# Two of the eight TensorE steps of the second modulation group are placed one wait earlier

## The reference, cut to what matters

```python
mod = jax.nn.silu(c) @ w_ada + b_ada                      # 1024 -> 6 * 1024
sh1, sc1, g1, sh2, sc2, g2 = split(mod, 6)
h = rms_norm(x, norm1_g) * (1 + sc1) + sh1
proj = h @ w_in                                            # qa, ka, va, qb, kb, vb, gates
qa, ka = rope(rms_norm(qa)), rope(rms_norm(ka))
for gi, (win, dil) in enumerate(DIL_GROUPS):               # 3 groups of 4 heads, head width 64
    o, l = dilated_window_attention(qa, ka, va, win, dil)
oa = sum(softmax(lses) * outs)                             # "first attention" of the kernel
ob = differential_attention(q1, q2, k1, k2, vb, lam)       # "second attention", 8 heads
x = x + g1 * ((gates_a * (oa @ w_proj_a) + gates_b * (ob @ w_proj_b)) @ w_out)
```

## Time and profile before

| what | us |
|---|---|
| median of three runs | 1869.84 |
| the profiled execution's own time | 1871.05 |
| its span, first to last instruction | 1869.3 |
| TensorE busy | 1827.0 |
| VectorE busy | 1371.7 |
| ScalarE busy | 912.0 |

### The profile page before, as it was taken

The page is one execution under the profiler, slowest core; times in us unless marked ns, Lnnn a source line. Parts: engine busy times, 40 slices in busy tenths (PEclk is TensorE's granted clock), DMA queues, the critical chain, the costliest instruction groups (busy, mean ns, idle before and its releaser), DMA issues.

```text
span 1869.3 us, 24560 instructions
## 1 busy us (share of the span) xinstructions
PE 1827.0 (98%) x9392; PEld 1530.4 (82%) x9392; DVE 1371.7 (73%) x1903; ACT 912.0 (49%) x1013; POOL 77.6 (4%) x101
## 2 busy tenths in 40 slices
PE   8999999999999999999999999999999999999998
PEld 4778766888899877888888888889988888888886
DVE  5679588669998665666666666667875688888897
ACT  2553465311334444444444444456645467667675
POOL 0000000100000431110000000000000000000000
PEclk9999899999999999999999999999999999999999
DMA  7655365434446785666555555555343589898884
GB/s 310 247 181 201 113 225 192 158 125 147 163 153 229 248 275 188 212 210 222 182 200 180 196 185 191 190 184 191 143 143 127 219 312 360 319 354 325 340 342 183
DMA packets 61697, 404.94 MB, mean 217 GB/s; under 512 B 8129, under 2 KB 8417, under 8 KB 15281
## 3 DMA queue, kind: packets, MB, share of 16 engines
q1 hardware_dynamic: 51904, 371.22, 54.2%
q0 software_dynamic: 5968, 20.82, 3.9%
q10 hardware_dynamic: 3746, 11.83, 1.9%
HBM read 391.25 MB, written 12.58 MB: 216 GB/s over the span
## 4 chain that ended last, share of the span: by engine, by line
PE 84%; DVE 7%; DMA 3%; ACT 3%; issue 1%; DVEq 0%; ACTq 0%; SPq 0%
PE ps L2339 18%; PE ps L2341 17%; PE ps L2340 17%; PE ps L2733 9%; PE ps L2451 7%; PE ps L2735 4%; PE ps L2761 3%; DVE wlo L1241 2%; DMA raw<-in_stream_dram 2%; ACT whi L693 2%; DMA BIG<-in_stream_dram 1%; PE ps L2942 1%; PE ps L2461 1%; PE ps L2563 1%; PE ps L2584 1%
## 5 line engine op out<-in xcount | busy, mean ns | idle before, releaser
L1241 DVE TENSOR_TENSOR wlo<-raw,whi 128x2048 fp32r<-128x2048 f32 x179 | 410.2, 2292 | 201.3 <-ACT whi L693 201.1
L693 ACT ACTIVATE whi<-raw 128x2048 fp32r<-128x2048 f32 x179 | 343.0, 1916 | 375.7 <-PE ps L2341 190.3
L2733 PE MATMUL ps<-tboth,whi 128*128 128x512 f32 x736 | 259.8, 398 | 0.0
L2339 PE MATMUL ps<-whi,phi 128*128 128x512 f32 x608 | 238.9, 393 | 6.2 <-DVE plo L1832 6.2
L2341 PE MATMUL ps<-whi,plo 128*128 128x512 f32 x608 | 237.4, 391 | 0.0
L2340 PE MATMUL ps<-wlo,phi 128*128 128x512 f32 x608 | 237.4, 391 | 0.0
L2339 PE MATMUL ps<-whi,tboth 128*128 128x512 f32 (+1 forms) x576 | 226.7, 394 | 7.0 <-DVE wlo L1241 4.2
L2341 PE MATMUL ps<-whi,tboth 128*128 128x512 f32 (+1 forms) x576 | 223.1, 387 | 0.0
L2340 PE MATMUL ps<-wlo,tboth 128*128 128x512 f32 (+1 forms) x576 | 223.0, 387 | 0.0
L2735 PE MATMUL ps<-tboth,wlo 128*128 128x256 f32 x644 | 181.0, 281 | 0.0
L2451 PE MATMUL ps<-h2T,raw 128*128 128x256 f32 x768 | 172.4, 380 | 0.0
(11 more groups left out here) (426 smaller groups left out, 3074.7 us busy)
## 6 DMA issues: line engine op xcount, KB each, us to landing
raw<-in_stream_dram SPq DMA_DIRECT2D x259, 1024.0 KB, 4.8
BIG<-in_stream_dram SPq DMA_DIRECT2D x84, 1024.0 KB, 6.6
BIG<-g_spill POOLq DMA_DIRECT2D x64, 128.0 KB, 4.8
BIG<-in_stream_dram SPq DMA_DIRECT2D x2, 2048.0 KB, 16.3
spare<-in_stream_dram SPq DMA_DIRECT2D x4, 1024.0 KB, 7.2
g_spill<-H ACTq DMA_DIRECT2D x4, 1024.0 KB, 4.8
g_spill<-MOD ACTq DMA_DIRECT2D x4, 1024.0 KB, 4.8
MID<-in_gains_dram POOLq DMA_DIRECT2D x7, 512.0 KB, 4.0
```

What stands on the lines that cost most here:

```text
L693: nc.scalar.activation(whi[:, u % 2, :], raw_of(u), ACT.Copy).then_inc(unit_hi, 1)
L1241: nc.vector.tensor_tensor(wlo[:, u % 2, :], raw_of(u), whi[:, u % 2, :].bitcast(f32), ALU.subtract).then_inc(unit_split, 1)
L2339: nc.tensor.matmul(out, ahi, bhi, start=start, stop=False)
L2733: last = nc.tensor.matmul(out, whi[:, s, cols], both, start=c == 0, stop=c == DC - 1)
```

## The change

`ada_half(1, 0)`, which stood behind the first two scores, now stands ahead of them, right behind the last transposes of q and k, with a wait for the copy that frees bank 7. `ada_half(1, 1)`, which stood in step 0 of the loop, takes the old place of `ada_half(1, 0)`. In the loop, step i now issues `ada_half(1, i + 2)` in place of `ada_half(1, i + 1)`, and step 6 issues none.

```diff
@@ -2545,6 +2545,9 @@
                 last.then_inc(qkT_done, 1)
+            pe.wait_ge(silu_spread, 1)
+            pe.wait_ge(qkT_odd, NQK // 4 * TT // 2 - 1)
+            ada_half(1, 0)
             pe.wait_ge(qkT_even, NQK // 4 * TT // 2)
             pe.wait_ge(qkT_odd, NQK // 4 * TT // 2)
@@ -2601,8 +2604,7 @@
             a_scores(0)
             a_scores(1)
-            pe.wait_ge(silu_spread, 1)
-            ada_half(1, 0)
+            ada_half(1, 1)
             for i in range(n_a):
                 a_transposes(i)
@@ -2611,8 +2613,8 @@
                 if i:
                     a_values(i - 1)
-                if i + 1 < DC:
-                    ada_half(1, i + 1)
+                if i + 2 < DC:
+                    ada_half(1, i + 2)
             a_values(n_a - 1)
```

## The result

Four runs of the changed kernel took 1901.33 to 1907.24 us, median 1903.08, beside 1868.28 us for the kernel before (1865.91 to 1872.03, four runs). The ratio is 1.0176, 95% interval 1.0147 to 1.0206: the change makes the kernel 1.5 to 2.1% slower, 33 us by the ratio. The forecast was 1899 us, range 1887 to 1905. The profiled execution after took 1901.33 us (span 1899.6), that of before 1871.05: 30.3 us more.

What follows compares the result with a forecast made beforehand. TensorE, busy in nearly every slice, was taken to bound the kernel. The first wait and five 10.3 us turns give 27.9 us, with the exit 29; 1871.05 + 29 = 1900.0, less 1.2 for the median: 1899 us, range 1887 to 1905.

Steps and rivals of the forecast that it cites:

- The two gaps: TensorE idle ahead of the first scores and during the first softmax: filling them costs 0 to 0.2 us, taken as 0.
- The wait at unit 2: Step 0 of the first attention: TensorE reaches ada_half(1, 2) at 214.42, unit 2 lands at 218.3, a wait of 3.9 us.
- The ring: First attention's loop: transposes, sum, load and ada_half become one path per step, 10.3 us a turn at half clock against 4.54.
- The clock: TensorE in the first attention's loop: 1.2 GHz taken for ada_half and transposes in every turn, because of waits of about 4 us.
- same ring, full clock: Rival in the first attention's loop: clock stays at 2.4 GHz, turns of 8.7 us, 19 us late, 1889 us; chance 0.17.
- The rule: Skill's pattern for the loop: matmuls shorter than the load wait lose the clock each time; turn 10.3 us, without it 8.7.
- The exit: End of first attention: sum of unit 7 follows step 6's transposes by 5.1 us, up to some 3 us more; 29 late.
- Behind the attention: Second attention and after: runs as before, so the first attention's delay of 29 us stays to the end.
- half clock runs on into the second attention: Rival in the second attention: each head at half clock costs 4.36 us more, time 1903 to 1908; chance 0.10.
- nothing gives the delay back: Second attention: the chain leaves through the load issued at 276.34, which follows a sum as well, so the delay stays.
- The median: Whole kernel: median of the runs taken 1.2 us below the profiled execution's 1900.0, hence 1899.
- The intended gain: First attention's loop: six ada_half in place of seven, worth 0.91 us at full clock and 1.81 at half.

Runs made afterwards that it cites:

- e1: Changed kernel with only the loop's order taken back, the two early steps kept: 1870.27 us, ratio 1.0006 to the kernel before.
- e4: Changed kernel with VectorE's sum of each unit put ahead of the reciprocal of the step, TensorE's order untouched: 1886.44 us, ratio 1.0102.
- e9: Changed kernel's TensorE order, with VectorE's sums one step earlier too: 1867.82 us, ratio 0.9999 to the kernel before.
- e5b: Changed kernel with 53 needless matmuls filling TensorE's waits, those of steps 1 to 5 ahead of the values: 1893.10 us, ratio 1.0138.
- e3: Changed kernel, but only units 2, 3 and 4 read one step early in the loop: 1886.39 us, ratio 1.0099 to the kernel before.
- e11: Kernel before with only VectorE's sums one step earlier, TensorE's order kept: 1866.44 us, ratio 0.9992.
- e7: Kernel before with only ada_half(1, 0) moved ahead of the first scores: 1870.37 us, ratio 1.0018.
- e10: As e9, with 4 extra matmuls behind ada_half(1, 1) in the wait for the first softmax: 1866.48 us, ratio 0.9988.
- e6: As e1, with 4 extra matmuls behind ada_half(1, 1) in the wait for the first softmax: 1869.09 us, ratio 0.9996.
- e8: Kernel before with 4 extra matmuls behind ada_half(1, 0) in the wait for the first softmax: 1866.74 us, ratio 0.9995.

## Why the prediction was right

**The two gaps.** Nearly right. The first scores start at 206.87, 0.35 us later than before (206.52). Of that, 0.24 us is that the transposes of q and k ended later (205.89, 205.65 before), which the change doesn't touch; the rest is within the 0 to 0.2 that bounded the cost of `ada_half(1, 0)`, though it was taken as 0.

**The wait at unit 2.** Right: forecast 3.9 us, measured 3.48 us, and released by the load. The issue of that load was 1.04 us later than taken (214.53, 213.49 before). The transposes of step 0, which lead to the sum of unit 0, started 0.38 us later (211.72, 211.34 before), and they took 1.54 us in place of 0.87, because the clock fell at about 211.8, under them; and the load took 5.0 us. Transposes of step 1: forecast 220.2, measured 221.46.

**The ring.** Right, term by term: one turn 10.3 us forecast, five turns 221.46 to 273.12 = 51.7 us measured, forecast 51.5. In the turn from 231.72 the terms were 3.58 us from the transposes to the issue, 4.91 for the load, 0.04 for TensorE to start and 1.87 for `ada_half`; 3.59, 4.8, 0.1 and 1.81 were taken. It was tested from three sides: without the loop's order (e1), without VectorE's part (e4), and with earlier loads under the same TensorE order (e9).

**The clock.** Right: half in every turn. e5b is the rival "same ring, full clock" made real, with the 8.7 us per turn that was worked out for it. The estimate for this rival was 19 us over before; e5b has 20 in its profiled execution, 26 by the ratio. In e3, where the clock recovered within each turn, it fell again in each of the three waits for a load (4.71, 3.70 and 3.75 us). In the changed kernel itself it didn't oscillate but stayed at half throughout, with waits of only 1.3 to 1.4 us after the first. The Trainium skill, "TensorE: Matmul & The Clock Gate", section "HAM oscillation — how this bites in real kernels", speaks of matmuls that are shorter than the wait for the next load. e3 agrees that the clock falls in each wait, but its matmuls were the longer part, 6.6 us from a wait to the next, and so were those of the turn at full clock in the prediction, 4.54 us beside about 4. The rule led to the right turn here without its condition being met, and the pattern of the changed kernel, half clock without oscillation, is another one. Why the clock stayed at half there isn't shown.

**The exit.** Forecast 5.1 to about 8 us from the transposes of step 6 to the sum of unit 7; measured 273.12 to 278.88 = 5.8, with the clock back at 276.6. The transposes of step 6 are 29.3 us late, where 27.9 was forecast, and the exit adds 0.7 us, where 1.1 was taken; part of the first error is cancelled by the second, by luck. The sum is 30.0 us late, 29 was taken.

**Behind the attention.** "As before" was a little wrong: the half-clock spell there lasted 6.8 us in place of 3.4 and covered the first `ada_half` of the third group, 3.19 us for what is 1.72 in a later head. The first matmul behind both attentions (L2339) starts at 325.43 in place of 294.14, so the delay grew there from 30.0 to 31.3 us: the rival in which half clock runs on into the second attention was real, with 1.3 us in place of 4.4 or more. The chain doesn't leave the second attention through a load as it did before, but through the work on its last heads (TensorE, ScalarE and VectorE in turn), so that reason for "nothing gives the delay back" was wrong; the delay stayed all the same, and at the end of the span it is 30.3 us.

**The median.** 1903.1 against 1899. Of these about 4 us, 1.3 are in the profiled execution (1901.33 against 1900.0). It was the fastest of the four, where the median had been taken to lie 1.2 us under it; the other three were 0.4 to 5.9 us slower, with clocks of 0.979 to 0.983 against 0.977, so the mean clock doesn't explain these microseconds, and there is no trace of them. That part stays open.

**The intended gain.** The sum had it right at 0.91 us in the loop (0.92 in e9 and e11). What it left out is that even without the ring unit 2's landing pins step 1 (e1).

## What to carry to other kernels

Before an operation that reads a streamed buffer is moved earlier, follow the path that frees the buffer: if the freeing work is itself behind the moved operation, the move shortens a ring of load, use and release, and each turn then costs the whole load, here 10.3 us in place of 4.5. Move the release (here the other engine's sum) by as many steps first. The idle time of the waits, 10.3 us here, is far less than the loss; count the turns of the chain, and price work behind a wait at the lower clock.

## What the runs showed of the hardware

- TensorE can be kept at 1.2 GHz for 64.5 us by a loop in which it is busy for 54.2 us of them (granted clock 0.50), with waits of 1.3 to 1.5 us per turn behind the first of 3.5. In the kernel before the clock was back at full after 13.6 us, in which TensorE had no wait.
- Useless matmuls in the waits buy time: e5b does more work than the changed kernel and takes 7 us less by the ratios, 10 by the medians; its clock was 1.00 in the stretch where that of the changed kernel was 0.50.
- A half-clock spell in or behind the first attention moves from trace to trace of nearly equal kernels: 212.8 to 226.4 before, 213.5 to 216.9 in e7, 211.4 to 218.3 in e9, 219.6 to 222.9 in e10, 248.5 to 251.9 in e6, none of these in e1, e8 and e11. Runs of one kernel differ by up to 17 us (e7, 1865.1 to 1882.4), more than any edit here could gain, and the slower ones have the lower mean clock (0.995 and 0.985 in these two).
